# Two transformer blocks on one core: the squares of the double norm are added by VectorE before TensorE sums them

## What is computed

```python
x = _rmsnorm(x + merged @ w_out, final_norm_g)            # end of the first block
h = modulate(rms_norm(x, norm_g[0]), shift[0], scale[0])  # begin of the second
x = x + 0.5 * gate[0] * swiglu(h, ffn1_w_in, ffn1_w_out)
```

## Time and profile before

| | us |
|---|---|
| runs of the kernel | 1952.11, 1955.33, 1955.80 |
| median | 1955.33 |
| profiled execution | 1952.12 |
| its span, first to last instruction | 1950.4 |
| TensorE busy | 1911.8 (98%) |
| VectorE busy | 1009.4 (52%) |
| ScalarE busy | 758.1 (39%) |
| POOL busy | 192.4 (10%) |
| chain that ended last: TensorE's share | 91% |

### The profile page before, as it was taken

One profiled execution on the slowest core, in us unless ns is written; L12 is line 12 of the kernel. 1 busy time (PEld: TensorE's weight loads), 2 busy tenths in 40 slices (PEclk: granted clock), 3 DMA queues, 4 the chain that ended last, 5 costly groups with the idle time before them and its releaser, 6 DMA issues.

```text
span 1950.4 us, 25821 instructions
## 1 busy us (share of the span) xinstructions
PE 1911.8 (98%) x9472; PEld 1577.2 (81%) x9472; DVE 1009.4 (52%) x1413; ACT 758.1 (39%) x1437; POOL 192.4 (10%) x242
## 2 busy tenths in 40 slices
PE   7999999999999999999999999999999999999998
PEld 5888868766788888888887788898888888888887
DVE  6788766565444563333344766544633573333332
ACT  4545533365523342222223664343522342222332
POOL 1101110000000000000011235035000000000010
PEclk9999999999999999999998999999999999999999
DMA  9967813211134323333333232211334323333331
GB/s 325 328 177 252 296 33 101 76 44 39 28 114 126 96 87 97 97 97 94 98 90 109 76 98 81 69 47 31 93 98 144 98 84 106 97 97 94 97 100 55
DMA packets 330904, 212.90 MB, mean 109 GB/s; under 512 B 21373, under 2 KB 315450, under 8 KB 330302
## 3 DMA queue, kind: packets, MB, share of 16 engines
q1 hardware_dynamic: 319830, 170.27, 30.2%
q0 software_dynamic: 10368, 37.75, 5.4%
q10 hardware_dynamic: 616, 3.67, 0.5%
HBM read 204.31 MB, written 7.35 MB: 109 GB/s over the span
## 4 chain that ended last, share of the span: by engine, by line
PE 91%; DVE 4%; DMA 2%; ACT 2%; issue 1%; SPq 0%; POOL 0%; DVEq 0%; POOLq 0%; ACTq 0%
PE psum L435 26%; PE psum L437 25%; PE psum L436 25%; PE psum L1483 2%; DMA ada_w<-in_ada_w 1%; PE psum L1269 1%; DVE ada_sum L2254 1%; PE psum L1301 1%; PE psum L1282 1%; DVE delta_qkv_T L2254 1%; PE psum L999 1%; PE psum L1001 1%; PE psum L1000 1%; PE psum L1183 1%; PE psum L1373 1%
## 5 line engine op out<-in xcount | busy, mean ns | idle before, releaser
L435 PE MATMUL psum<-act_hi,w_hi 128*128 128x512 f32 x1616 | 648.1, 401 | 4.8 <-DVE act_lo L2254 2.5
L437 PE MATMUL psum<-act_hi,w_lo 128*128 128x512 f32 x1616 | 630.7, 390 | 0.0
L436 PE MATMUL psum<-act_lo,w_hi 128*128 128x512 f32 x1616 | 630.3, 390 | 0.0
L394 DVE TENSOR_TENSOR w_lo<-w_raw,w_hi 128x1024 fp32r<-128x1024 f32 x306 | 384.1, 1258 | 318.1 <-ACT w_hi L386 296.1
L386 ACT ACTIVATE w_hi<-w_raw 128x1024 fp32r<-128x1024 f32 x306 | 319.4, 1052 | 180.6 <-PE psum L437 173.4
L435 PEld LDWEIGHTS psum<-act_hi,w_hi 128*128 128x128 f32 x1616 | 303.9, 188 | 83.6 <-issue 20.0
L437 PEld LDWEIGHTS psum<-act_hi,w_lo 128*128 128x128 f32 x1616 | 303.7, 188 | 65.0
L436 PEld LDWEIGHTS psum<-act_lo,w_hi 128*128 128x128 f32 x1616 | 304.2, 188 | 60.6 <-issue 1.4
L770 POOL TENSOR_TENSOR squares<-squares 128x512 f32<-128x512 f32 x18 | 28.9, 1605 | 1237.2 <-ACT squares L1671 1237.2
L435 PE MATMUL psum<-ffn_hi,w_hi 128*128 128x512 f32 (+1 forms) x374 | 141.7, 379 | 0.0
L437 PE MATMUL psum<-ffn_hi,w_lo 128*128 128x512 f32 (+1 forms) x374 | 140.9, 377 | 0.0
(11 more groups left out here) (370 smaller groups left out, 2359.2 us busy)
## 6 DMA issues: line engine op xcount, KB each, us to landing
w_raw<-in_ffn_w_in SPq DMA_DIRECT2D x88, 512.0 KB, 3.7
ada_w<-in_ada_w POOLq DMA_DIRECT2D x72, 512.0 KB, 5.4
w_raw<-in_w_in SPq DMA_DIRECT2D x68, 512.0 KB, 3.8
w_raw<-in_mix_w_in SPq DMA_DIRECT2D x52, 512.0 KB, 3.7
w_raw<-in_ffn_w_out SPq DMA_DIRECT2D x32, 512.0 KB, 4.0
w_raw<-in_ffn_w_out SPq DMA_DIRECT2D x16, 384.0 KB, 3.2
w_raw<-in_w_branch_a SPq DMA_DIRECT2D x8, 512.0 KB, 3.9
w_raw<-in_w_out SPq DMA_DIRECT2D x8, 512.0 KB, 4.0
```

Source lines behind the costliest of these rows:

```text
L394: dve.tensor_tensor(WLO[:, n % 4, :], RAW[:, n % 4, :], WHI[:, n % 4, :].bitcast(F32), ALU.subtract).then_inc(w_lo, 1)
L435: pe.matmul(out, whi, hhi, start=start, stop=False)
L436: pe.matmul(out, whi, hlo, start=False, stop=False)
L437: return pe.matmul(out, wlo, hhi, start=False, stop=stop)
```

## The change

`double_sum` is no longer called after each tile of out1. VectorE keeps two running sums instead: the squares themselves in slot 0 of SQ, and the squares times g² in UTMP, a tile of 128x512 that is otherwise used later. `add_squares(k)`, for k = 0 to 6, stands between `raw_lo(k)` and the split of the next chunk; k = 0 is one operation (SQ's slot 0 is the running sum already, UTMP gets the product), each other k is an addition and a multiply-and-add. After kk = 1 of `raw_pair(1)` TensorE sums the two running sums over the partitions with four matmuls of one column each, and the last feature tile with four of two columns as before. ScalarE's slots for the squares are the same for all norms now, and its wait for a slot is on VectorE's additions. The thresholds of the semaphores `squares_added` (now counted by VectorE for the double norm, then by POOL) and `square_sum` are renumbered for it.

```diff
--- before.py
+++ after.py
@@ -540,7 +540,7 @@
 
         def square_slot(r, k):
 
-            return k % 4 if r == DOUBLE else 1 + (k - 1) % 3
+            return 1 + (k - 1) % 3 if k else 0
 
         def turned_by(u):
 
@@ -766,7 +766,7 @@
                 for k in range(1, KD - 1):
                     pool.wait_ge(sem("squares_ready"), NT + 8 * (r - 1) + k + 1)
                     if k > 1:
-                        pool.wait_ge(sem("squares_added"), 6 * (r - 2) + k - 1)
+                        pool.wait_ge(sem("squares_added"), 6 * (r - 1) + k - 1)
                     pool.tensor_tensor(SQ[:, 0, :], SQ[:, 0, :], SQ[:, square_slot(r, k), :], ALU.add)\
                         .then_inc(sem("squares_added"), 1)
 
@@ -851,22 +851,27 @@
                     mm = pe.transpose(PS[:, 4 + k % 3, n * P:n * P + P], XTOK[:, n, k * P:k * P + P], ID)
                 mm.then_inc(sem("x_T"), 1)
 
-            def double_sum(k):
-
-                pe.wait_ge(sem("squares_ready"), NT + k + 1)
+            def double_sum():
+
+                pe.wait_ge(sem("squares_added"), 6)
+                for t, sums in enumerate((SQ[:, 0, :], UTMP[:])):
+                    for n in range(NT):
+                        pe.matmul(PS[:, 4, NT * t + n:NT * t + n + 1], sums[:, n * P:n * P + P], ONES[:, 0:1],
+                                  start=(t == 0 and n == 0), stop=False)
+                pe.wait_ge(sem("squares_ready"), NT + KD)
                 for n in range(NT):
-                    mm = pe.matmul(PS[:, 4, n:n + NT + 1:NT], SQ[:, square_slot(DOUBLE, k), n * P:n * P + P],
-                                   SQW[:, k, :], start=(k == 0 and n == 0), stop=(k == KD - 1 and n == NT - 1))
+                    mm = pe.matmul(PS[:, 4, n:n + NT + 1:NT], SQ[:, square_slot(DOUBLE, KD - 1), n * P:n * P + P],
+                                   SQW[:, KD - 1, :], start=False, stop=(n == NT - 1))
                 mm.then_inc(sem("square_sum"), 1)
 
             def rms_sum(r):
 
                 if r == DOUBLE:
-                    double_sum(KD - 1)
+                    double_sum()
                     return
                 for part in range(2):
                     if part == 0:
-                        pe.wait_ge(sem("squares_added"), 6 * (r - 1))
+                        pe.wait_ge(sem("squares_added"), 6 * r)
                     else:
                         pe.wait_ge(sem("squares_ready"), NT + 8 * r)
                     first = 0 if part == 0 else square_slot(r, KD - 1)
@@ -915,8 +920,6 @@
                     for k in range(first, pl.nb):
                         pe_tile(pe, pl, k, k, kts, rhi, rlo, act_ready=ready if k == 0 else None)
                         mods(name, k, pl)
-                        if name == "out1" and k:
-                            double_sum(k - 1)
                 stage(name, body)
 
             def first_pair(tiles, base):
@@ -1048,7 +1051,7 @@
             def last_sums(half, part):
 
                 if part == 0:
-                    pe.wait_ge(sem("squares_added"), 6 * 3)
+                    pe.wait_ge(sem("squares_added"), 6 * 4)
                     if half:
                         pe.wait_ge(sem("mean_recip"), NT + 4)
                 else:
@@ -1661,14 +1664,9 @@
             def square(r, k):
 
                 act.wait_ge(x_ready, NORM_X[r] - 8 + k + 1)
-                if r == DOUBLE:
-                    if k >= 4:
-                        act.wait_ge(sem("square_sum"), k - 3)
-                    e = act.activation(SQ[:, square_slot(r, k), :], XT[:, k, :], ACT.Square)
-                else:
-                    if k >= 4:
-                        act.wait_ge(sem("squares_added"), 6 * (r - 2) + k - 3)
-                    e = act.activation(SQ[:, square_slot(r, k) if k else 0, :], XT[:, k, :], ACT.Square)
+                if k >= 4:
+                    act.wait_ge(sem("squares_added"), 6 * (r - 1) + k - 3)
+                e = act.activation(SQ[:, square_slot(r, k), :], XT[:, k, :], ACT.Square)
                 e.then_inc(sem("squares_ready"), 1)
                 if r in RAW_AT:
                     act.activation(HHI[:, k, :], XT[:, k, :], ACT.Copy, scale=col(COEF_OF[r] + k)).then_inc(sem("h_hi"), 1)
@@ -1678,7 +1676,7 @@
                 for half in range(2):
                     tok = slice(256 * half, 256 * half + 256)
                     act.wait_ge(x_ready, NORM_X[4] + half)
-                    act.wait_ge(sem("squares_added"), 6 * 2 + KD - 1 - 3)
+                    act.wait_ge(sem("squares_added"), 6 * 3 + KD - 1 - 3)
                     act.activation(SQ[:, square_slot(4, KD - 1), tok], XT[:, KD - 1, tok], ACT.Square)\
                        .then_inc(sem("squares_ready"), 1)
                     act.wait_ge(sem("squares_ready"), NT + 8 * 4 + half)
@@ -2292,7 +2290,7 @@
 
                 base = H_AT[r]
 
-                dve.wait_ge(sem("square_sum"), KD + 2 * (r - 1))
+                dve.wait_ge(sem("square_sum"), 1 + 2 * (r - 1))
                 chained(ts(col(RCOL, 4), PS[:, 4, 0:NT], 1.0 / D, EPS, ALU.mult, ALU.add))
                 if r == DOUBLE:
 
@@ -2695,12 +2693,24 @@
                 ins = dve.tensor_reduce(BSUM[:, t, :], BPART[:].rearrange("p (k n) -> p n k", n=P), AX, ALU.add)
                 chained(ins) if t == 0 else ins.then_inc(sem("bias_parts"), 1)
 
+            def add_squares(k):
+
+                dve.wait_ge(sem("squares_ready"), NT + k + 1)
+                sq = SQ[:, square_slot(DOUBLE, k), :]
+                if k == 0:
+                    chained(ts(UTMP[:], sq, SQW[:, 0, 1:2], None, ALU.mult))
+                    return
+                chained(tt(SQ[:, 0, :], SQ[:, 0, :], sq, ALU.add))
+                stt(UTMP[:], sq, SQW[:, k, 1:2], UTMP[:], ALU.mult, ALU.add).then_inc(sem("squares_added"), 1)
+
             def residual(name, per_tile, gate_col, normed=False, r=None):
 
                 pl = Place(name, 0)
                 for f in range(KD):
                     if r and f:
                         raw_lo(r, f - 1)
+                    if r == DOUBLE and f:
+                        add_squares(f - 1)
                     for c in range(per_tile):
                         split_lo(dve, pl, per_tile * f + c + AHEAD)
                         if c == 0 and normed:
@@ -3012,7 +3022,7 @@
                 chained(stt(XT[:, f, tok], PS[:, pl.bank(f + half), tok], col(MOD + 48 + 16 + f), XT[:, f, tok], ALU.mult, ALU.add))
                 dve.sem_inc(x_ready, 1)
                 rcol = col(RCOL + 2 * half, 2)
-                dve.wait_ge(sem("square_sum"), KD + 2 * 2 + 1 + half)
+                dve.wait_ge(sem("square_sum"), 1 + 2 * 2 + 1 + half)
                 chained(ts(rcol, PS[:, 4, mine], 1.0 / D, EPS, ALU.mult, ALU.add))
                 dve.reciprocal(rcol, rcol).then_inc(sem("mean_recip"), 1)
                 dve.wait_ge(sem("rms_ready"), NT + 4 + half)
```

## The result

| | before | changed |
|---|---|---|
| median of 22 runs, us | 1954.47 | 1957.17 |
| lowest run, us | 1950.79 | 1952.41 |
| profiled span, us | 1950.4 | 1955.2 |

The ratio is 1.0015, 95% interval 1.0009 to 1.0021: 2.9 us slower, 1.8 to 4.1. That is less than the 0.2% which the prediction took for what a measurement can tell; over 22 and 21 runs it is distinct from nothing. (One run of the changed kernel took 2755 us and is left out of the ratio.)

A forecast was written before the change was run, and what follows sets the result against it. The prediction took TensorE, busy throughout out1, as the bound. A gain of 2.64 us left after its stand, 1.80 for added matmuls and 1.5 for low clock gave +0.7; added to the median 1955.33 this made 1956.0 us, range 1951.5 to 1959.5.

The forecast's parts named there:

- Removed from TensorE: In out1, seven blocks of sum-of-squares matmuls go, after tiles 1 to 7, 0.95 us each: 6.65 us less.
- Added to TensorE: Behind kk = 1 of raw_pair, twelve matmuls in place of four, 16 records more: 1.80 us on the path.
- Added to VectorE: In out1, add_squares between raw_lo and split costs 1.40 us per pair, 0.55 for k = 0: 8.95 us.
- Does it fit: VectorE finishes chunk 9 late, so TensorE stands 3.89 us before raw_pair; 2.64 of the 6.65 us are left.
- The clock: Behind TensorE's stand before raw_pair, the granted clock is low: 1.5 us lost, bounds 0 and 3.0.
- Rival 4: TensorE's low clock holds for two stretches: +2.2 us, 1957.5, no change; chance 0.06.
- Rival 1: TensorE stands before raw_pair but the clock stays full: -0.84 us, 1954.5, no change; chance 0.17.
- Rival 2: VectorE keeps up in out1, chunk 9 split by 679.6: -4.85 us, 1950.5, just faster; chance 0.07.
- Rival 3: At add_squares the passes slow each other or neighbours, 0.5 us longer each: +6.7 us, 1962; chance 0.08.

The follow-up runs named there:

- e8: Changed kernel with five feature tiles of raw_pair's first output tile, then the running sums' 16 records, before the wait for chunk 9; ratio 0.9973 to the kernel before.
- e6: Changed kernel with the running sums' 16 records behind kk = 0 of raw_pair, the last feature tile's 8 behind kk = 1; ratio 1.0024 to the kernel before.
- e4: Kernel before with VectorE's two passes per tile added into scratch tiles, nothing taken from TensorE; ratio 1.0001 to the kernel before.
- e10: Changed kernel with add_squares behind the split of the next chunk in place of ahead of it; ratio 0.9998 to the kernel before.
- e7: Changed kernel with POOL adding the plain running sum and VectorE keeping only the weighted one; ratio 1.0007 to the kernel before.
- e9: Kernel before with only raw_pair reordered, five feature tiles of its first output tile first; ratio 1.0003 to the kernel before.
- e1: Changed kernel without VectorE's passes: add_squares only counts, TensorE reads slot 0 of SQ twice; ratio 0.9976 to the kernel before.
- e3: Changed kernel with raw_pair reordered: five feature tiles of its first output tile before the wait for chunk 9; ratio 0.9981 to the kernel before.
- e11: Repeat of e8, the changed kernel with first tile early and sum split; ratio 0.9977 to the kernel before.
- e2: Changed kernel with 16 useless 128x512 matmuls at the start of raw_pair, waiting for chunk 8 only; ratio 0.9999 to the kernel before.

## Why the prediction was right, and where it was off

The forecast was no change, 1956.0 within 1951.5 to 1959.5; 1957.17 came. Against the kernel before it was +0.7 us by its sum and 2.9 measured. The absolute time came out nearer, 1.2 us off, only because the median of three runs to which the sum was added, 1955.33, lay 0.9 above the median of 22; that is luck. Point by point:

- **Removed from TensorE**, -6.65 us: right. In e8 the pair starts 6.62 us earlier (35.79 behind the memset for 42.41).
- **Added to TensorE**, 1.80 us: right, 2.62 - 0.80 = 1.82. A record costs 2.62 / 24 = 0.109 us at full clock, and in the window of the sum TensorE's 24 weight loads are busy for all of its 2.62 us: each record has a load of its own. The Trainium skill (TensorE: Matmul & The Clock Gate, section LDWEIGHTS) prices a load by its columns over 1.2 GHz, an estimate of 0.107 us for 128. At full clock the trace agrees with that, and not with the issue floor that the prediction cited; at the low clock of e6 it doesn't, with 3.27 / 16 = 0.204 us a record.
- **Added to VectorE**, 1.40 a pair: right, 1.39. The scalar multiply cost 0.52 and not 0.55. e4 shows that the passes cost nothing by themselves.
- **Does it fit**: right. The chain was off by 0.12 us of 36. The stand was 3.72 for 3.89, and 3.87 when counted as the prediction does, from when out1's last matmul would have let the next one start (681.67) to 685.54.
- **The clock**, 1.5 us: here the sum failed. The term was 3.99 in the first profile and 3.15 in the second (2.39 + 1.60, 1.55 + 1.60). That the clock would be low behind the stand was right, but rows 7 didn't show it: there the clock was low before the stand of 2.47 us (0.50 from 1054.0 to 1055.5, with TensorE busy), and stands of 2.27 and 2.80 us amid dense work cost no clock (e10, e7). Two things were missing in the size. The stretch behind the stand cost 2.39 us in one execution and 1.55 in the other. And the longer sum brings a low stretch of its own, 1.6 us, in six of the seven profiles that have 24 such records in a row, while the three with eight records (before, e4, e9) have none; e1 shows that it needs no stand. The price of the added matmuls was taken as their length alone. Rival 4 came nearer with two stretches (+2.2), but without the sum as the cause of one.
- **Rival 1** (full clock behind the stand) holds for stands of 2.3 and 2.8 us (e10, e7), not for 3.7. **Rival 2** (-4.85) didn't occur; it is the time of e1 by the runs (-4.7) and of e8. **Rival 3** didn't occur with POOL idle; e7 shows that its mechanism is real once POOL works beside VectorE.

What stays open: why e3 shows no low clock behind its 24 records. It has more wide matmuls ahead of them (21 in place of 12) and one profile only, so either the order or the execution may be the reason. Whether the length of the run of narrow matmuls decides isn't shown either: e6, which was to cut it in two, was low from the stand on, and e8 and e11, which cut it too, have e3's order. The Trainium skill (TensorE: Matmul & The Clock Gate, Part 1) says that the number of matmuls at the low level differs between runs of one kernel; the two profiles of the changed kernel, with 2.39 and 1.55 us lost behind the same stand, agree. Whether it is this that spreads the changed kernel's runs wasn't tried by itself.

## What to carry to other kernels

A helper that had idle time while the bounding engine did the work may have none once that work is taken away: compare the added work with the waits in the new, shorter period, and follow the helper's chain to the next thing that the bounding engine waits for. Where it comes out late, put work that needs less in front of the wait (e8), or the new work behind what is waited for (e10, which here only gave back the loss). Count a stand of TensorE, and also a long run of its narrow matmuls, with the low clock that may follow.

## What was not expected of the hardware

- Eight narrow f32 matmuls in a row, 1.70 us, left the clock full behind out2 (rows 5). Twelve (24 records), 2.62 us, were followed by 1.6 us lost at 1.2 GHz in e1, e2, e7 and e10, where the twelve wide matmuls ahead of them ran at full clock.
- Stands of 2.27 and 2.80 us amid dense work didn't lower the clock, in one profile each. Stands of 3.72 us did in two of two, for 2.39 and 1.55 us of loss, and one of 3.95 did (e6). In the first profile the clock fell inside the stand of 3.72, in the second 0.7 us behind its end.
- At the low clock the narrow matmuls cost nearly twice their time as well (0.204 us a record for 0.109), and in e6 the stretch stayed low for most of 21 us.
- Beside POOL's addition of 128x512 VectorE's `raw_lo` of 0.75 us took 1.28 or 1.67 and ended 0.54 to 0.56 us behind it (e7).
